# SwiGLU expansions: products of 512 columns into a pair of banks, from the fourth chunk on

## The chip, the core and the metric

The kernel runs on one core of a Trainium2 chip. The metric is the device time in microseconds. Three runs of the kernel before gave 1954.67 us as their median (1953.87 to 1956.11).

## What is computed

The reference is a stack of transformer-like blocks over 256 positions of width 1024 in fp32: two layers of a first kind (attention and gated linear attention, a recurrent mixer, convolution FFNs) and then two layers of a second kind. The change touches the second kind only, and there the two SwiGLU networks of each layer:

```python
def swiglu(h, w_gate_up, w_down):
    gu = h @ w_gate_up                      # 1024 -> 2 x 2816
    g, u = jnp.split(gu, 2, axis=-1)
    return (jax.nn.silu(g) * u) @ w_down    # 2816 -> 1024

for l in range(DEPTH):                      # DEPTH = 2
    h = swiglu(rms_norm_2(x, ffn1_pre[l]), ffn1_w_gate_up[l], ffn1_w_down[l])
    x = x + 0.5 * rms_norm_2(h, ffn1_post[l])
    h = hybrid_mixer(rms_norm_2(x, mix_pre[l]), ...)
    x = x + rms_norm_2(h, mix_post[l])
    h = swiglu(rms_norm_2(x, ffn2_pre[l]), ffn2_w_gate_up[l], ffn2_w_down[l])
    x = x + 0.5 * rms_norm_2(h, ffn2_post[l])
```

## The kernel before

Activations lie transposed: 128 channels on the partitions, 256 positions along the free side. A layer's input is 8 such tiles (`KT`), the hidden side of a SwiGLU 22 (`FF2`).

**Weights** come as one stream of chunks in the order of use. A chunk is 16 blocks of 128x128 (1 MB): in an expansion ("up") the 8 input tiles times two output tiles, one of `g` and one of `u`. SyncE moves it into one of three raw buffers (`w_raw`), as soon as VectorE has finished with the chunk three before it. ScalarE rounds it to a high part (`w_hi`, L213), VectorE takes the rest (`w_lo`, L222); both are rings of four chunks. At the end of chunk c ScalarE rounds chunk c + 4 (`refill_hi`) and VectorE makes the rest of chunk c + 3 (`refill_lo`).

**A product** is made in three parts, since fp32 values are split into a high and a low half: high weights by high input, high weights by low input, low weights by high input. The input's halves lie side by side in `x_split` (`xs`), high then low, 256 columns each; the hidden tiles in `h_split` (`hs`) likewise. `multiply` (L240 to L242) issues three matmuls of 256 columns for each block, all into the same half of a bank: both output tiles of a chunk share one PSUM bank. `multiply_wide` (L255, L258) issues one matmul of 512 columns (high weights by both halves) and one of 256 (low weights by the high half) for each block; it needs a bank for each output tile, whose left and right halves must be added afterwards. It is used in the first three of the four column groups of the contractions ("down").

**Banks.** Four PSUM banks rotate. Each use is an event; event e waits until event e - 4 has been taken by VectorE (the semaphore `pair_taken`, which starts at 4; `taken(e)` waits for the taking of e itself).

**An up stage** has 22 chunks. The layer's norm is computed while its first three chunks are multiplied: chunks 0 and 1 go together (`alternating`, L277 and L284), chunk 2 has two small matmul groups of the norm between its blocks (L316, L338), and only then is the inverse rms (`rinv`) there, by which `take_scaled` (L296) multiplies a chunk's bank while it copies it to `scratch`. From chunk 3 on TensorE goes by `whole_pe`. ScalarE works through `up_act`: for each chunk a rounding (L213), the silu of `g` (L610) and the high half of the hidden tile two chunks back (L616). VectorE works through `up_dve`: L296, the rest (L222), silu times `u` of the chunk before (L662) and the low half of the tile two back (L668).

The four stages in question are called upA and upB, in layers 0 and 1. In the profiled execution chunk 3 of them starts at 723, 1146, 1344 and 1767 us. upA and upB are each followed by a down stage of the same name.

Of the kernel before, what the change touches and what calls it, by code (L numbers as in the profile page):

```python
# [26 lines left out]
P = 128  # L27
T = 256
# [10 lines left out]
LEVELS = 8  # L39

# [4 lines left out]
LAYER = [("upA", FF2, FF2), ("downA", 12, 7), ("bg", 4, 4), ("pool_in", 4, 4), ("cv", 8, 8),  # L45
         ("gates", 8, 8), ("conv_out", 4, 4), ("pool", 1, 4), ("pool_out", 4, 4),
         ("w_o", 4, 4), ("upB", FF2, FF2), ("downB", 12, 7)]
# [96 lines left out]
class Chunk:  # L144


    def __init__(self, phase, n, layer=0):
        self.n, self.buf = n, n % 3
        self.number = C0[phase] + n + layer * LAYER_CHUNKS
        self.slot = self.number % RING  # L150
        self.event = E0[phase] + n + layer * LAYER_EVENTS
        self.bank = self.event % BANKS

# [7 lines left out]
def program(nc, x_in, stream, par1_in, par2_in, ev_const, mask_const, mats, inv_in, out):  # L161
    with ExitStack() as ctx:
# [37 lines left out]
        pair_taken = sem("psum_pair_taken")  # L200
        const_landed = sem("const_landed")
# [47 lines left out]
        def multiply_wide(pe, c, banks, src, k0, nk, first, last, ready):  # L249

            for k in range(nk):
                pe.wait_ge(*ready(k0 + k))
                for m, bank_ in enumerate(banks):
                    b = (k * 2 + m) * P
                    pe.matmul(ps[:, bank_, :], w_hi[:, c.slot, b:b + P],  # L255
                              src[:, k0 + k, :, :].rearrange("p a t -> p (a t)"),
                              start=first and k == 0, stop=False)
                    done = pe.matmul(tile(bank_, 0), w_lo[:, c.slot, b:b + P], src[:, k0 + k, 0, :],  # L258
                                     start=False, stop=last and k == nk - 1)
            done.then_inc(chunk_done, 1)  # L260
# [32 lines left out]
        def take_scaled(dve, c, dst, tiles=2):  # L293

            dve.wait_ge(chunk_done, c.number + 1)
            dve.tensor_tensor(dst, bank(c.bank, tiles), rinv[:, :].unsqueeze(1).to_broadcast([P, tiles, T]),  # L296
                              ALU.mult).then_inc(pair_taken, 1)
# [61 lines left out]
        def pre_pe(pe, phases, tr, summed, l):  # L359

            for ph, n in phases:
                done = 0
                if ph == phases[0][0]:
                    alternating(pe, Chunk(ph, 0, l), Chunk(ph, 1, l), xs, KT,
                                lambda k: tr["hi"].count(k + 1, l), lambda k: tr["lo"].count(k + 1, l))
                    c = Chunk(ph, 2, l)
                    pe.wait_ge(pair_taken, c.event + 1)
                    pe.wait_ge(lo_ready, c.number + 1)
                    multiply(pe, c, pair_tiles(c.bank), xs, 0, KT, True, True, signal=(chunk_done, 1),
                             hooks={0: lambda: mean_pe(pe, tr, summed, l), 4: lambda: rinv_pe(pe, tr, l)})  # L370
                    done = 3
                whole_pe(pe, ph, n, l, done)

        def whole_pe(pe, ph, n, l, done=0):
            for c in chunks(ph, n, l, done):
                pe.wait_ge(pair_taken, c.event + 1)
                pe.wait_ge(lo_ready, c.number + 1)
                multiply(pe, c, pair_tiles(c.bank), xs, 0, KT, True, True, signal=(chunk_done, 1))
# [224 lines left out]

        def up_act(act, phase, n, tr, func, conv, pre, l):


            def gate(c, prev):
                s = (c.slot - prev) % RING
                act.wait_ge(*(tr["gate"].count(c.n + 1 - prev, l) if conv else taken(c.event - prev)))
# [18 lines left out]
            for c in chunks(phase, n, l):  # L628
                at = c.n
                act.wait_ge(chunk_done, c.number + 1)  # L630
                if at == 0:
# [1332 lines left out]
```

## Time and profile before

| | |
|---|---|
| Median of three runs | 1954.67 us (1953.87 to 1956.11) |
| The profiled execution, time | 1953.41 us |
| The profiled execution, span of the trace | 1951.6 us |
| TensorE matmul busy | 1880.3 us, 96% |
| TensorE weight loads busy | 1821.2 us, 93% |
| VectorE busy | 1350.0 us, 69% |
| ScalarE busy | 933.8 us, 48% |
| Granted clock of TensorE, mean over the span | 0.974 |

The span is the time from the first to the last instruction in the trace. Matmuls are pipelined: a row's duration overlaps that of its neighbours, and the pace of the engine is seen from start to start.

### The profile page before, as it was taken

To read this page: it belongs to the slowest core of one execution; us is meant where nothing else is said; L and a number is where in the kernel's file an instruction comes from. 1 tells how busy PE (TensorE), PEld (TensorE's weight loads), DVE (VectorE), ACT (ScalarE), POOL (GpSimd) and SP (SyncE) were. 2 spreads that over 40 slices of the span, in tenths; PEclk is the share of its full clock that TensorE was granted. 3 is DMA by queue.
4 is the path that set the end of the run, shared out by engine and by line. 5 is a ranking of instruction groups with operands and counts; after the bars stand their busy time and mean duration, and the time that the engine had idled before them with its cause. 6 is when DMAs were issued, how large, how long until landed. Compare 5 with 4: busy or idle time off the path is not lost.

```text
span 1951.6 us, 34117 instructions
## 1 busy us (share of the span) xinstructions
PE 1880.3 (96%) x14532; PEld 1821.2 (93%) x14532; DVE 1350.0 (69%) x1676; ACT 933.8 (48%) x1101; POOL 134.0 (7%) x119
## 2 busy tenths in 40 slices
PE   7959999998999999999999999999999999999997
PEld 7938999898999899989999999999999999999997
DVE  5796899568799566656775676657665686576564
ACT  5443665457666444444354454435444445344442
POOL 0000333000233000000300000000000020000000
PEclk9968999999999999999999999999999999989999
DMA  7312555534455545553455444553555445445551
GB/s 282 145 43 76 174 193 193 185 141 164 177 200 176 192 152 178 190 215 138 166 199 190 173 151 175 205 203 133 192 187 208 145 172 196 151 152 194 186 203 66
DMA packets 46797, 334.82 MB, mean 172 GB/s; under 512 B 5184, under 2 KB 5568, under 8 KB 6464
## 3 DMA queue, kind: packets, MB, share of 16 engines
q1 hardware_dynamic: 46512, 332.20, 47.6%
q8 instruction: 115, 1.88, 0.4%
q0 software_dynamic: 144, 0.52, 0.1%
q14 instruction: 26, 0.21, 0.0%
HBM read 331.65 MB, written 1.05 MB: 170 GB/s over the span
## 4 chain that ended last, share of the span: by engine, by line
PE 88%; DVE 7%; ACT 2%; issue 1%; DMA 1%; SPq 0%; ACTq 0%; DVEq 0%
PE psum L240 19%; PE psum L241 19%; PE psum L242 19%; PE psum L255 10%; PE psum L277 7%; PE psum L258 5%; PE psum L284 3%; DVE w_lo L222 2%; PE psum L316 1%; DVE scratch L1282 1%; PE psum L483 1%; DMA w_raw<-stream_in 1%; PE psum L486 1%; PE psum L485 1%; PE psum L338 1%
## 5 line engine op out<-in xcount | busy, mean ns | idle before, releaser
L213 ACT ACTIVATE w_hi<-w_raw 128x2048 fp32r<-128x2048 f32 x313 | 598.4, 1914 | 707.5 <-PE psum L242 451.6
L240 PE MATMUL psum<-x_split,w_hi 128*128 128x256 f32 x2984 | 848.1, 284 | 11.1 <-DVE x_split L354 10.5
L241 PE MATMUL psum<-x_split,w_hi 128*128 128x256 f32 x2984 | 845.1, 283 | 0.0
L242 PE MATMUL psum<-x_split,w_lo 128*128 128x256 f32 x2984 | 845.0, 283 | 0.0
L222 DVE TENSOR_TENSOR w_lo<-w_raw,w_hi 128x2048 fp32r<-128x2048 f32 x313 | 717.4, 2296 | 55.7 <-ACT w_hi L213 55.7
L240 PEld LDWEIGHTS psum<-x_split,w_hi 128*128 128x128 f32 x2984 | 573.5, 192 | 12.3 <-issue 11.2
L241 PEld LDWEIGHTS psum<-x_split,w_hi 128*128 128x128 f32 x2984 | 573.6, 192 | 0.1
L242 PEld LDWEIGHTS psum<-x_split,w_lo 128*128 128x128 f32 x2984 | 573.4, 192 | 0.0
L296 DVE TENSOR_TENSOR scratch<-psum,inv_rms 128x512 f32<-128x512 f32 (+1 forms) x205 | 139.6, 687 | 240.7 <-PE psum L242 240.5
L255 PE MATMUL psum<-h_split,w_hi 128*128 128x512 f32 x816 | 288.6, 399 | 0.0
L258 PE MATMUL psum<-h_split,w_lo 128*128 128x256 f32 x816 | 229.2, 281 | 0.0
L255 PEld LDWEIGHTS psum<-h_split,w_hi 128*128 128x128 f32 x816 | 153.4, 188 | 38.0
L258 PEld LDWEIGHTS psum<-h_split,w_lo 128*128 128x128 f32 x816 | 154.2, 189 | 0.0
L240 PE MATMUL psum<-h_split,w_hi 128*128 128x256 f32 x448 | 126.9, 283 | 2.0 <-issue 2.0
L241 PE MATMUL psum<-h_split,w_hi 128*128 128x256 f32 x448 | 126.8, 283 | 0.0
L242 PE MATMUL psum<-h_split,w_lo 128*128 128x256 f32 x448 | 126.8, 283 | 0.0
L678 DVE SCALAR_TENSOR_TENSOR scratch<-scratch,params 128x255 f32<-128x255 f32 x192 | 120.5, 687 | 5.0 <-ACT scratch L624 4.3
L543 DVE COPY scratch<-psum 128x256 f32<-128x256 f32 (+1 forms) x42 | 18.3, 459 | 119.4 <-PE psum L258 67.4
L277 PE MATMUL psum<-x_split,w_hi 128*128 128x256 f32 x288 | 82.6, 318 | 9.5 <-ACT x_split L349 9.5
L240 PEld LDWEIGHTS psum<-h_split,w_hi 128*128 128x128 f32 x448 | 86.0, 192 | 2.5 <-issue 2.2
L242 PEld LDWEIGHTS psum<-h_split,w_lo 128*128 128x128 f32 x448 | 86.0, 192 | 0.0
L241 PEld LDWEIGHTS psum<-h_split,w_hi 128*128 128x128 f32 x448 | 86.0, 192 | 0.0
(204 smaller groups left out, 1892.7 us busy)
## 6 DMA issues: line engine op xcount, KB each, us to landing
w_raw<-stream_in SPq DMA_DIRECT2D x313, 1024.0 KB, 4.8
x_resid<-x_in SPq DMA_DIRECT2D x1, 1024.0 KB, 7.0
y_out<-x_resid SPq DMA_DIRECT2D x4, 256.0 KB, 2.5
scratch<-mask_in SPq DMA_DIRECT2D x1, 768.0 KB, 10.9
scratch<-ev_in SPq DMA_DIRECT2D x1, 512.0 KB, 9.5
scratch<-inv_in POOLq DMA_DIRECT2D x1, 512.0 KB, 3.9
params<-par_in SPq DMA_DIRECT2D x1, 247.0 KB, 7.1
matrices<-mat_in SPq DMA_DIRECT2D x1, 192.0 KB, 8.9
```

What stands on the lines that cost most here:

```text
L213: act.activation(w_hi[:, n % RING, :], raw[:, n % RAWS, :], ACT.Copy).then_inc(hi_ready, 1)
L222: dve.tensor_tensor(w_lo[:, n % RING, :], raw[:, n % RAWS, :], w_hi[:, n % RING, :].bitcast(F32), ALU.subtract).then_inc(lo_ready, 1)
L240: pe.matmul(dst, w_hi[:, c.slot, b:b + P], src[:, k0 + k, 0, :], start=opens, stop=False)
L241: pe.matmul(dst, w_hi[:, c.slot, b:b + P], src[:, k0 + k, 1, :], start=False, stop=False)
L242: done = pe.matmul(dst, w_lo[:, c.slot, b:b + P], src[:, k0 + k, 0, :], start=False, stop=last and k == nk - 1 and m == len(tiles_) - 1)
L255: pe.matmul(ps[:, bank_, :], w_hi[:, c.slot, b:b + P], src[:, k0 + k, :, :].rearrange("p a t -> p (a t)"), start=first and k == 0, stop=False)
L258: done = pe.matmul(tile(bank_, 0), w_lo[:, c.slot, b:b + P], src[:, k0 + k, 0, :], start=False, stop=last and k == nk - 1)
L277: pe.matmul(tile(c.bank, m), w[:, c.slot, b:b + P], src[:, k0 + k, 0, :], start=k == 0 and m == 0 and w is w_hi, stop=False)
L284: done = pe.matmul(tile(c.bank, m), w_hi[:, c.slot, b:b + P], src[:, k0 + k, 1, :], start=False, stop=k == nk - 1 and m == 1)
L296: dve.tensor_tensor(dst, bank(c.bank, tiles), rinv[:, :].unsqueeze(1).to_broadcast([P, tiles, T]), ALU.mult).then_inc(pair_taken, 1)
L316: ins = pe.matmul(ps[:, 7, h:h + 1], part[:, h * P:(h + 1) * P], ONES[:, 0:1], start=opens and n == 0 and h == 0, stop=closes and n == len ...
L678: dve.scalar_tensor_tensor(out=scr[:, ACC + 2 * s + t, d:T], in0=scr[:, PRE + 2 * s + t, 0:T - d], scalar=conv[0][:, bass.ds(((c.n - prev) ...
```

## The change

In the up stages of the second block (`WIDE`), chunks 3 to 21 (`NARROW = 3`) are multiplied with `multiply_wide` instead of `multiply`. Such a chunk takes two events and so two banks. When it is done, ScalarE copies the right halves of both banks into `scratch` (`ACC`, semaphore `up_right`), VectorE adds them to the left halves and releases both banks, and then multiplies the sum by `rinv` in place (semaphore `up_scaled`). The silu of a wide chunk waits for `up_scaled`. Chunks 0 to 2, the first block's expansions and all other stages are as they were.

```diff
+NARROW = 3
+WIDE = ("upA", "upB")
...
-LAYER = [("upA", FF2, FF2), ("downA", 12, 7), ...
+LAYER = [("upA", FF2, 2 * FF2 - NARROW), ("downA", 12, 7), ...
...
-        self.event = E0[phase] + n + layer * LAYER_EVENTS
+        self.wide = phase in WIDE and n >= NARROW
+        self.event = E0[phase] + n + layer * LAYER_EVENTS + (n - NARROW if self.wide else 0)
         self.bank = self.event % BANKS
+        self.last = self.event + 1 if self.wide else self.event
...
         def take_scaled(dve, c, dst, tiles=2):
 
             dve.wait_ge(chunk_done, c.number + 1)
+            if c.wide:
+                dve.wait_ge(up_right, wide_count(c))
+                dve.tensor_tensor(dst, ps[:, c.bank:c.bank + 2, 0:T], S(ACC + 2 * c.slot, 2),
+                                  ALU.add).then_inc(pair_taken, 2)
+                dve.wait_ge(*taken(c.last))
+                dve.tensor_tensor(dst, dst, rinv[:, :].unsqueeze(1).to_broadcast([P, 2, T]),
+                                  ALU.mult).then_inc(up_scaled, 1)
+                return
...
         def whole_pe(pe, ph, n, l, done=0):
             for c in chunks(ph, n, l, done):
-                pe.wait_ge(pair_taken, c.event + 1)
+                pe.wait_ge(pair_taken, c.last + 1)
                 pe.wait_ge(lo_ready, c.number + 1)
-                multiply(pe, c, pair_tiles(c.bank), xs, 0, KT, True, True, signal=(chunk_done, 1))
+                whole(pe, c)
+
+        def whole(pe, c, hooks={}):
+            if c.wide:
+                multiply_wide(pe, c, (c.bank, c.bank + 1), xs, 0, KT, True, True, hooks=hooks)
+            else:
+                multiply(pe, c, pair_tiles(c.bank), xs, 0, KT, True, True, signal=(chunk_done, 1), hooks=hooks)
...
+        def scaled(c):
+            if c.wide:
+                return up_scaled, wide_count(c)
+            return taken(c.event)
...
-                act.wait_ge(*(tr["gate"].count(c.n + 1 - prev, l) if conv else taken(c.event - prev)))
+                act.wait_ge(*(tr["gate"].count(c.n + 1 - prev, l) if conv else scaled(Chunk(phase, c.n - prev, l))))
...
             for c in chunks(phase, n, l):
                 at = c.n
                 act.wait_ge(chunk_done, c.number + 1)
+                if c.wide:
+                    act.activation(S(ACC + 2 * c.slot, 2), ps[:, c.bank:c.bank + 2, T:2 * T], ACT.Copy)\
+                       .then_inc(up_right, 1)
```

How the instructions stand now. VectorE at the start of upA in layer 0, before, from the first taking after the norm on; L296 is the multiply out of PSUM, L222 the low weights, L662 and L668 the hidden tile:

```order
L296 TENSOR_TENSOR scratch<-psum,inv_rms 128x512 [waits chunk_multiplied,normA_stat]
L296 TENSOR_TENSOR scratch<-psum,inv_rms 128x512 [waits chunk_multiplied] x2
L222 TENSOR_TENSOR w_lo<-w_raw,w_hi 128x2048 [waits chunk_hi_ready]
L662 TENSOR_TENSOR scratch<-scratch 128x256 [waits upA_act_ready] x2
L668 TENSOR_TENSOR h_split<-scratch,h_split 128x256 [waits upA_hi_ready]
L296 TENSOR_TENSOR scratch<-psum,inv_rms 128x512 [waits chunk_multiplied]
L222 TENSOR_TENSOR w_lo<-w_raw,w_hi 128x2048 [waits chunk_hi_ready]
```

And the same place now; the line numbers are those of the changed kernel, and `up_right_halves_copied` is ScalarE's copy:

```order
L313 TENSOR_TENSOR scratch<-psum,inv_rms 128x512 [waits chunk_multiplied,normA_stat]
L313 TENSOR_TENSOR scratch<-psum,inv_rms 128x512 [waits chunk_multiplied] x2
L228 TENSOR_TENSOR w_lo<-w_raw,w_hi 128x2048 [waits chunk_hi_ready]
L695 TENSOR_TENSOR scratch<-scratch 128x256 [waits upA_act_ready] x2
L701 TENSOR_TENSOR h_split<-scratch,h_split 128x256 [waits upA_hi_ready]
L307 TENSOR_TENSOR scratch<-psum,scratch 128x512 [waits up_right_halves_copied,chunk_multiplied]
L310 TENSOR_TENSOR scratch<-scratch,inv_rms 128x512 [waits psum_pair_taken]
L228 TENSOR_TENSOR w_lo<-w_raw,w_hi 128x2048 [waits chunk_hi_ready]
```

The first three chunks are taken as before; from chunk 3 on two instructions stand where one stood, ahead of the low weights.

ScalarE at the same place, chunks 2 and 3, before:

```order
L213 ACTIVATE w_hi<-w_raw 128x2048 [waits chunk_landed_1,chunk_multiplied]
L610 ACTIVATE scratch<-scratch 128x256 [waits psum_pair_taken]
L616 ACTIVATE h_split<-scratch 128x256 [waits upA_hidden_ready]
L213 ACTIVATE w_hi<-w_raw 128x2048 [waits chunk_landed_2,chunk_multiplied]
L610 ACTIVATE scratch<-scratch 128x256 [waits psum_pair_taken]
```

And now:

```order
L219 ACTIVATE w_hi<-w_raw 128x2048 [waits chunk_landed_1,chunk_multiplied]
L640 ACTIVATE scratch<-scratch 128x256 [waits psum_pair_taken]
L646 ACTIVATE h_split<-scratch 128x256 [waits upA_hidden_ready]
L662 ACTIVATE scratch<-psum 128x512 [waits chunk_multiplied]
L219 ACTIVATE w_hi<-w_raw 128x2048 [waits chunk_landed_2]
L640 ACTIVATE scratch<-scratch 128x256 [waits up_pair_scaled]
```

The copy (L662) stands ahead of the rounding, and the silu (L640) waits for VectorE's second step.

## Rows read from the trace of the kernel before

**Rows 1.** The page: busy time by engine, and the chain that ended last.

```profile
PE 1880.3 (96%) x14532; PEld 1821.2 (93%) x14532; DVE 1350.0 (69%) x1676; ACT 933.8 (48%) x1101; POOL 134.0 (7%) x119
...
PE 88%; DVE 7%; ACT 2%; issue 1%; DMA 1%; SPq 0%; ACTq 0%; DVEq 0%
```

**Rows 2.** Busy time by stretch, inside upA, layer 0; last: clock, DMA share, GB/s.

```profile
735.00:830.00 95.00, 95.00 (x794) 95.00 (x793) 59.70 (x66) 42.95 (x51) 0.00 (x0) 1.00 0.53 185
```

**Rows 3.** All waits of the same stretch: total us, times, longest.

```profile
ACT w_hi L213 <- PE psum L242: 55.0, 17, 3.2
DVE scratch L296 <- PE psum L242: 37.4, 17, 2.2
```

**Rows 4.** Timeline, TensorE (start us, us): chunk 3 and the down stage's first matmul.

```profile
723.39 0.28 PE L240 MATMUL psum<-x_split,w_hi 128*128 128x256 f32 x1
...
832.83 0.40 PE L255 MATMUL psum<-h_split,w_hi 128*128 128x512 f32 x1
...
1145.64 0.28 PE L240 MATMUL psum<-x_split,w_hi 128*128 128x256 f32 x1
...
1255.08 0.40 PE L255 MATMUL psum<-h_split,w_hi 128*128 128x512 f32 x1
...
1767.03 0.28 PE L240 MATMUL psum<-x_split,w_hi 128*128 128x256 f32 x1
...
1876.47 0.40 PE L255 MATMUL psum<-h_split,w_hi 128*128 128x512 f32 x1
```

**Rows 5.** Timeline, TensorE, down stage of layer 0 and the end of its third group.

```profile
847.32 0.40 PE L255 MATMUL psum<-h_split,w_hi 128*128 128x512 f32 x1
847.56 0.28 PE L258 MATMUL psum<-h_split,w_lo 128*128 128x256 f32 x1
847.67 0.40 PE L255 MATMUL psum<-h_split,w_hi 128*128 128x512 f32 x1
...
879.47 0.28 PE L240 MATMUL psum<-h_split,w_hi 128*128 128x256 f32 x1
879.59 0.28 PE L241 MATMUL psum<-h_split,w_hi 128*128 128x256 f32 x1
```

**Rows 6.** Groups of instructions (busy us, mean ns, idle before), shapes near the new ones.

```profile
L401 ACT ACTIVATE scratch<-x_resid 128x512 f32<-128x512 f32 x24 | 13.1, 616 | 0.0
L1020 ACT ACTIVATE scratch<-psum,params 128x256 f32<-128x256 f32 x16 | 6.2, 516 | 0.0
L1571 DVE TENSOR_TENSOR scratch<-scratch 128x512 f32<-128x512 f32 x8 | 5.5, 692 | 0.3
L1543 DVE TENSOR_TENSOR scratch<-psum,scratch 128x512 f32<-128x512 f32 x8 | 5.5, 690 | 23.1 <-PE psum L284 16.8 <-PE psum L242 6.4
```

**Rows 7.** Timeline, ScalarE, one chunk of upA, layer 0.

```profile
821.51 1.92 ACT L213 ACTIVATE w_hi<-w_raw 128x2048 fp32r<-128x2048 f32 x1 [3.23 <-PE psum L242]
823.33 0.40 ACT L610 ACTIVATE scratch<-scratch 128x256 f32<-128x256 f32 x1
```

**Rows 8.** Timeline, VectorE: an add and the one that waits for it.

```profile
708.08 0.68 DVE L429 TENSOR_TENSOR square_sum<-scratch 128x512 f32<-128x512 f32 x1
708.87 1.49 DVE L429 TENSOR_TENSOR square_sum<-square_sum,scratch 128x512 f32<-128x512 f32 x2
```

**Rows 9.** Timeline, VectorE, one chunk of upA, layer 0, and the last hidden tile.

```profile
821.51 0.69 DVE L296 TENSOR_TENSOR scratch<-psum,inv_rms 128x512 f32<-128x512 f32 x1 [2.20 <-PE psum L242]
822.12 2.28 DVE L222 TENSOR_TENSOR w_lo<-w_raw,w_hi 128x2048 fp32r<-128x2048 f32 x1
...
836.85 0.99 DVE L668 TENSOR_TENSOR h_split<-scratch,h_split 128x256 fp32r<-128x256 f32 x2
```

**Rows 10.** Transfers of the stretch 735 to 830: KB each, median us to landing.

```profile
w_raw<-stream_in SPq DMA_DIRECT2D x16, 1024.0 KB, 4.8
```

**Rows 11.** Timeline, VectorE: chunks 0 to 2 of upA, layer 0, taken.

```profile
722.38 1.90 DVE L296 TENSOR_TENSOR scratch<-psum,inv_rms 128x512 f32<-128x512 f32 x3
```

More of the change, by code:

```diff
@@ L44 @@
          ("up1", FF1, FF1), ("down1", 12, 7)]
-LAYER = [("upA", FF2, FF2), ("downA", 12, 7), ("bg", 4, 4), ("pool_in", 4, 4), ("cv", 8, 8),
+LAYER = [("upA", FF2, 2 * FF2 - NARROW), ("downA", 12, 7), ("bg", 4, 4), ("pool_in", 4, 4), ("cv", 8, 8),
          ("gates", 8, 8), ("conv_out", 4, 4), ("pool", 1, 4), ("pool_out", 4, 4),
-         ("w_o", 4, 4), ("upB", FF2, FF2), ("downB", 12, 7)]
+         ("w_o", 4, 4), ("upB", FF2, 2 * FF2 - NARROW), ("downB", 12, 7)]
 C0, E0 = {}, {}
@@ L147, in __init__ @@
     def __init__(self, phase, n, layer=0):
-        self.n, self.buf = n, n % 3
+        self.n, self.buf, self.phase, self.layer = n, n % 3, phase, layer
         self.number = C0[phase] + n + layer * LAYER_CHUNKS
         self.slot = self.number % RING
-        self.event = E0[phase] + n + layer * LAYER_EVENTS
+        self.wide = phase in WIDE and n >= NARROW
+        self.event = E0[phase] + n + layer * LAYER_EVENTS + (n - NARROW if self.wide else 0)
         self.bank = self.event % BANKS
+        self.last = self.event + 1 if self.wide else self.event
 def chunks(phase, count, layer=0, done=0):
@@ L200, in program @@
         pair_taken = sem("psum_pair_taken")
+        up_scaled = sem("up_pair_scaled")
+        up_right = sem("up_right_halves_copied")
         const_landed = sem("const_landed")
@@ L247, in multiply, with multiply_wide @@
                 done.then_inc(*signal)
-        def multiply_wide(pe, c, banks, src, k0, nk, first, last, ready):
+        def multiply_wide(pe, c, banks, src, k0, nk, first, last, ready=None, hooks={}):
             for k in range(nk):
-                pe.wait_ge(*ready(k0 + k))
+                if ready is not None:
+                    pe.wait_ge(*ready(k0 + k))
                 for m, bank_ in enumerate(banks):
@@ L259, in multiply_wide @@
                                      start=False, stop=last and k == nk - 1)
+                if k in hooks:
+                    hooks[k]()
             done.then_inc(chunk_done, 1)
@@ L366, in pre_pe @@
                     c = Chunk(ph, 2, l)
-                    pe.wait_ge(pair_taken, c.event + 1)
+                    pe.wait_ge(pair_taken, c.last + 1)
                     pe.wait_ge(lo_ready, c.number + 1)
-                    multiply(pe, c, pair_tiles(c.bank), xs, 0, KT, True, True, signal=(chunk_done, 1),
-                             hooks={0: lambda: mean_pe(pe, tr, summed, l), 4: lambda: rinv_pe(pe, tr, l)})
+                    whole(pe, c, hooks={0: lambda: mean_pe(pe, tr, summed, l), 4: lambda: rinv_pe(pe, tr, l)})
                     done = 3
@@ L375, in whole_pe @@
             for c in chunks(ph, n, l, done):
-                pe.wait_ge(pair_taken, c.event + 1)
+                pe.wait_ge(pair_taken, c.last + 1)
                 pe.wait_ge(lo_ready, c.number + 1)
-                multiply(pe, c, pair_tiles(c.bank), xs, 0, KT, True, True, signal=(chunk_done, 1))
+                whole(pe, c)
[4 more added lines that the diff above has]
+                multiply(pe, c, pair_tiles(c.bank), xs, 0, KT, True, True, signal=(chunk_done, 1), hooks=hooks)
         def post_tracks(name, layered=True):
@@ L602, in up_tracks, with wide_count @@
             return {k: Signal(sem(f"{name}_{k}_ready"), 2 * m if k == "taps" else m) for k in names}
+        def wide_count(c):
+            return (WIDE.index(c.phase) + 2 * c.layer) * (FF2 - NARROW) + c.n - NARROW + 1
+        def scaled(c):
+            if c.wide:
+                return up_scaled, wide_count(c)
+            return taken(c.event)
         def up_act(act, phase, n, tr, func, conv, pre, l):
```

## The prediction, made before the changed kernel was run

> **What bounds the kernel now.** I read the page first: TensorE is busy for 1880.3 of 1951.6 us, VectorE for 1350.0, ScalarE for 933.8, and 88% of the chain that ended last is TensorE [rows 1]. A busy share does not say which wait ends last in the part that is changed, so the second view is the stretch table inside the first changed stage, upA of layer 0. There TensorE is busy without a break, 95.00 of 95.00 us, at a granted clock of 1.00, while VectorE has 59.70 and ScalarE 42.95 us of work [rows 2]. The third view is the list of waits of the same stretch: only two kinds of waits stand there, and in both another engine waits for TensorE [rows 3]. So in this stage the time is the number of TensorE instructions times their spacing, and nothing else, as long as the others stay in time.
>
> **What a product costs, from start to start.** A matmul's own 0.28 us in the rows overlaps its neighbours, so I take starts. Chunk 3 of the stage (the first that is changed) begins at 723.39 and the down stage's first matmul at 832.83 [rows 4]. Between them lie 19 chunks of 16 blocks (8 input tiles by 2 output tiles), each block three products of 256 columns: 109.44 / 19 = 5.760 us a chunk, / 16 = 0.3600 us a block, 0.120 us a product. The other three stages read the same: 1145.64 to 1255.08 for the second and 1767.03 to 1876.47 for the fourth, 109.44 us each [rows 4], and the third likewise. So there is no stall in any of the four that the change could take away; it can gain only by a cheaper block.
>
> The down stage right behind is already written in the new form, one product of 512 columns and one of 256 for a block. Its first three groups run from 832.83 to 879.47 [rows 4, 5]: 46.64 us for 3 groups x 22 tiles x 2 = 132 blocks, 0.3533 us a block. One period can be read singly: 847.32, 847.56, 847.67, that is 0.24 and 0.11 to 0.12 us [rows 5]. The number of streamed columns is 768 in both forms; what goes is one instruction and one weight load a block.
>
> **The change part by part.**
>
> TensorE, the gain. 4 stages x 19 chunks x 16 blocks = 1216 blocks; the order listing has 1216 products of 512 columns on x_split where before had 2 x 1216 of 256. Each saves 0.3600 - 0.3533 = 0.0067 us: 0.107 us a chunk (5.760 to 5.653), 2.03 us a stage, **8.1 us in all**. Both figures are from blocks that read the same kind of ring slots and the same layout of high and low halves; only the moving buffer differs (x_split for h_split). The bounds of this term: nothing saved, 0.3600; and on the other side the 768 columns alone at the granted full clock, 2.4 GHz, 0.320 us, which would save 48.6 us. The down stage's row is the same code (multiply_wide) with the same shapes, so I take 0.3533.
>
> What the skill would make of it: the Trainium skill, page "TensorE: Matmul & The Clock Gate", section "Back-to-back issue gap", gives a warm matmul N / 2.4 + 2.5 ns. By that a dropped instruction returns only its fixed 2.5 ns, 1216 x 2.5 ns = 3.0 us in all, an estimate from that page. The trace disagrees with the page: 256 columns take 120 ns here and not 109, and the pair returns 6.7 ns.
>
> ScalarE, one more instruction a chunk: the copy of the right halves, 128x512 out of PSUM. No such row is there; the nearest are a 128x512 activation out of SBUF, 616 ns, and a 128x256 one out of PSUM, 516 ns [rows 6]. I take 0.61, bounds 0.52 and 1.0 (twice the smaller). In the steady stage ScalarE is idle for 3.23 us of each 5.76 [rows 7], so this is hidden; the copy stands ahead of the rounding of the next weights (w_hi, L213) and delays it by about 0.5 us. Behind that stands the silu (L610), which now waits for VectorE's second step; it comes up 0.61 + 1.82 = 2.4 us after the old start of the rounding [rows 7], and VectorE's result is there by 2.3 (below).
>
> VectorE: L296 (one multiply by the inverse rms out of PSUM) becomes an add of PSUM and scratch and a multiply in scratch, both 128x512: 690 and 692 ns [rows 6]. The multiply waits for the add itself. Such a dependent step costs 0.79 us from start to start (708.08 to 708.87) [rows 8], where L222 follows L296 after 0.61 [rows 9]. Of that 0.11 lies between the end of the one and the start of the other, and I take it for the copy's signal too. So, counted from where L296 started before: the copy 0.61 and its signal 0.11, then the add (ends at 1.41), the multiply 0.79 after its start (ends at 2.20), w_lo 0.61 behind that, 0.72 + 0.79 + 0.61 = 2.12 us where it was 0.61. VectorE is later by 1.51 us a chunk. It was idle for 2.20 us a chunk [rows 9], and the chunk is 0.11 shorter: 0.58 us of idle is left. So it keeps up, without a backlog that grows. What is queued behind the new wait: w_lo of the chunk three further on, the product of silu and up (L662), and the low half of the hidden tile (L668).
>
> Who waits for that. (1) The banks: a wide chunk takes two of the four, so chunk n needs the add of chunk n-2, which ends 1.41 us after that chunk's end and is wanted 5.65 after it. (2) w_lo: made at a chunk's end for the chunk that starts two chunks later, 11.3 us; it is ready after 4.4. (3) The raw weights: their buffer is freed 1.51 us later. Before, w_lo ended at 824.40 [rows 9], a transfer lands 4.8 us on [rows 10], 829.2, and the rounding that wants it is two chunks after 821.51 [rows 7], 833.03: 3.8 us to spare, and then 3.8 - 1.51 - 0.21 + 0.61 = 2.7. (4) The down stage: it wants the last hidden tile (k = 21) at its 43rd block, 847.67 [rows 5]; VectorE made it by 836.85 + 0.99 = 837.84 [rows 9], now about 1.5 later, 8 us ahead. All four are hidden; cost 0.
>
> The start of the stage. Chunk 3 used to wait for a bank of the stage before; now it needs two banks and so the taking of chunk 0. VectorE does that first of three, from 722.38 [rows 11], so until about 723.07, and chunk 3 starts at 723.39 [rows 4], its first weights 0.12 earlier: 0.2 us to spare. That is the thinnest place. Cost 0 as read; at the other bound TensorE runs dry for 0.3 us and picks up again, in four stages 1.2 us. Chunk 4 needs chunk 2, taken by 722.38 + 1.90 = 724.28 [rows 11], 5 us ahead.
>
> Fewer instructions and another parity of the banks in later stages: the banks only rotate, and nobody waits for them there beyond the same chain; 0.
>
> **Sum.** The profiled execution: 1953.41 us around a span of 1951.6. Less 8.1: 1945.3 and 1943.5. The median of the runs, 1954.67, lies 1.26 above the profiled one; less 8.1 it is **1946.6**.
>
> **The rivals.**
>
> A. A block with x_split as the moving operand costs more than 0.3568 us, so that less than 3.9 us is left. For it: no row shows 512 columns of x_split, and the up stage has more reads of PSUM by the other engines. Against it: in products of 256 columns x_split and h_split cost the same, 0.120 us (879.47 to 879.59 [rows 5] beside the 0.120 of the up stage), with and without a wait for each tile. The mechanism would be that the dropped instruction returns only part of the 13 ns by which 120 exceeds 256 columns at full clock. Between 1950.8 and 1954.7; if it returned only a fifth, 1216 x 0.0026 = 3.2, 1951.5. By the page's rule above the time would be 1951.6. Chance 6%, since 132 blocks beside it show the whole 6.7.
>
> B. Slower: VectorE becomes the bound of the wide chunks. It decides where its chain for a chunk is over 5.65 us; my sum is 5.07 (5.76 - 2.20 + 1.51). A lateness L per chunk adds up over 19 chunks; the first 4.2 us of it (5.65 - 1.41) are taken up before chunk n waits for the add of n-2. To turn the gain of 8.1 into a loss of 3.9, 3.0 us a stage must be lost: 19 L = 7.2, L = 0.38, a chain of 6.0 us, 1.0 more than the rows give: a copy that takes 1.6 us, or a multiply with a broadcast operand in place at over twice its 0.69. The time would be 1958.6 or more. Against it: all of these operations have rows of nearly the same shape. 3%.
>
> C. TensorE stalls at chunk 3 because the taking of chunk 0 is 0.2 us too close: 0.3 to 0.6 us in each of four stages, 1947.8 to 1949.0. Inside the forecast's range, still faster. 12% of the 90% below.
>
> D. Much faster, towards 0.320 us a block: 1% or less, since the down rows are the same code. That the change does not do what it says is excluded by the listing.
>
> **How the numbers follow.** Forecast 1946.6 with its variants 90%, A 6%, B 3%, D 1%. The forecast's own width: the runs before spread over 2.2 us (1953.87 to 1956.11), so 1.1 to each side for the median and as much for the 8.1, and C on the upper side: 1944.3 to 1950.0. That holds about 88%, and I leave A and B out. A measurement of this kernel can tell about 0.2%, 3.9 us, from no change: faster by more than that is under 1950.8, so 91%; within it 6%; slower 3%.
>
> **What would show it.** Right: in the four up stages from chunk 3 on, 0.353 us a block and 5.65 us a chunk, 107.4 us from chunk 3 to the down stage; TensorE busy throughout; new rows of about 0.61 us on ScalarE and 0.69 twice on VectorE; VectorE idle ahead of the add for 0.6 us a chunk by its own queue plus the wait for the copy; every later stage of unchanged length and only shifted by 2, 4, 6 and 8 us. Wrong: a block of 0.357 or more (A); rows in which TensorE waits for the add of VectorE in the middle of a stage (B) or once at chunk 3 (C); a ScalarE wait for a transfer in the up stages, which has none now.

## The result and the profile after

The changed kernel takes **1940.91 us** (three runs, 1940.50 to 1941.37) where the kernel before took 1954.67: ratio 0.9933, 95% interval 0.9913 to 0.9952. The forecast was 1946.6 with a range of 1944.3 to 1950.0. It is faster, as forecast, but by 13.8 us in place of 8.1, and below the range. The profiled execution took 1940.91 us around a span of 1939.1, 12.5 us less than that of before (1953.41, 1951.6). Among all later runs, two executions were slower by far more than any other (one of `before_late4`, 2273.85 us, and one of the kernel before beside it, 3634.54), and they are left out of every median here.

The page of the changed kernel, busy time by engine (beside [rows 1]), then the stretch table inside upA of layer 0, beside [rows 2], and all waits from 726 to 830 us, beside [rows 3]:

```profile
PE 1868.7 (96%) x13316; PEld 1751.0 (90%) x13316; DVE 1403.1 (72%) x1752; ACT 971.5 (50%) x1177; POOL 133.7 (7%) x119
```

```profile
735.00:830.00 95.00, 95.00 (x540) 82.42 (x540) 71.27 (x84) 51.20 (x68) 0.00 (x0) 1.00 0.53 188
```

```profile
ACT scratch L662 <- PE psum L265: 46.1, 18, 2.7
DVE scratch L307 <- ACT scratch L662: 24.6, 18, 1.4
DVE h_split L701 <- ACT h_split L646: 1.0, 1, 1.0
```

TensorE is still busy for 95.00 of 95.00 us, VectorE now for 71.27 and ScalarE for 51.20, and apart from TensorE only ScalarE is waited for, by VectorE: in each chunk for the copy, 1.37 us (24.6 / 18), and once for a hidden tile. The timeline of TensorE at chunk 3 of that stage, at the end of the stage, and where the third group of the down stage ends, beside [rows 4, 5] (start us, duration us):

```profile
724.22 0.28 PE L248 MATMUL psum<-x_split,w_lo 128*128 128x256 f32 x1
724.34 0.40 PE L262 MATMUL psum<-x_split,w_hi 128*128 128x512 f32 x1
...
831.64 0.28 PE L265 MATMUL psum<-x_split,w_lo 128*128 128x256 f32 x1
831.75 0.40 PE L262 MATMUL psum<-h_split,w_hi 128*128 128x512 f32 x1
...
878.39 0.28 PE L246 MATMUL psum<-h_split,w_hi 128*128 128x256 f32 x1
```

From chunk 3 to the down stage it is 831.75 - 724.34 = 107.41 us, 0.3533 us a block; the forecast said 107.4 and 0.353. The other three stages read 107.41, 107.42 and 107.41. Chunk 3 starts 0.12 us behind the last product of chunk 2 in all four, so there is no stall. VectorE and ScalarE in one chunk of the same stage, beside [rows 9] and [rows 7]:

```profile
815.72 0.69 DVE L307 TENSOR_TENSOR scratch<-psum,scratch 128x512 f32<-128x512 f32 x1 [1.36 <-ACT scratch L662]
816.45 0.69 DVE L310 TENSOR_TENSOR scratch<-scratch,inv_rms 128x512 f32<-128x512 f32 x1
817.06 2.28 DVE L228 TENSOR_TENSOR w_lo<-w_raw,w_hi 128x2048 fp32r<-128x2048 f32 x1
```

```profile
814.99 0.60 ACT L662 ACTIVATE scratch<-psum 128x512 f32<-128x512 f32 x1 [2.64 <-PE psum L265]
815.49 1.91 ACT L219 ACTIVATE w_hi<-w_raw 128x2048 fp32r<-128x2048 f32 x1
817.30 0.40 ACT L640 ACTIVATE scratch<-scratch 128x256 f32<-128x256 f32 x1
```

The copy takes 0.60 us (forecast 0.61). The add starts 0.73 behind its start (0.72), the multiply 0.73 behind that (0.79), and w_lo 2.07 us after the copy's start (2.12). All of it is hidden.

**Where the other 4.4 us of the profile are.** Between two stages lies a *norm passage*: behind the last product of the contraction come the norm's own small matmuls and the first two chunks of the next stage, which TensorE takes as their inputs arrive. I count it from the start of TensorE's last product of the contraction to the start of its first product of chunk 2. There are six of them behind each other from 698 us on, before and after built alike. This is the stretch table of the six of before; the numbers behind the colon are the length, and the third from the end is the mean granted clock:

```profile
698.11:716.31 18.20, 15.82 (x111) 15.38 (x110) 13.37 (x23) 7.87 (x15) 0.00 (x0) 0.81 0.15 46
896.08:914.21 18.13, 15.78 (x112) 15.34 (x111) 15.27 (x28) 8.28 (x15) 0.00 (x0) 0.81 0.02 3
1120.12:1138.56 18.44, 16.09 (x112) 15.76 (x110) 15.98 (x28) 8.28 (x15) 0.00 (x0) 0.81 0.06 13
1318.33:1336.65 18.32, 15.97 (x111) 15.64 (x110) 15.87 (x28) 8.27 (x15) 0.00 (x0) 0.81 0.05 8
1516.42:1534.69 18.27, 15.92 (x111) 15.59 (x110) 15.82 (x28) 8.27 (x15) 0.00 (x0) 0.81 0.03 4
1740.72:1759.95 19.23, 16.88 (x111) 16.45 (x110) 15.85 (x28) 8.27 (x15) 0.00 (x0) 0.73 0.05 9
```

And the same six of the changed kernel:

```profile
699.14:717.26 18.12, 15.74 (x111) 15.30 (x110) 13.37 (x23) 7.87 (x15) 0.00 (x0) 0.81 0.13 45
895.00:912.26 17.26, 14.91 (x112) 14.58 (x111) 14.80 (x28) 8.28 (x15) 0.00 (x0) 0.90 0.00 1
1118.10:1136.31 18.21, 15.86 (x112) 15.53 (x111) 15.75 (x28) 8.29 (x15) 0.00 (x0) 0.81 0.06 15
1314.05:1331.91 17.86, 15.52 (x111) 15.08 (x110) 14.89 (x28) 8.28 (x15) 0.00 (x0) 0.81 0.01 1
1509.65:1526.78 17.13, 14.78 (x111) 14.45 (x110) 14.67 (x28) 8.27 (x15) 0.00 (x0) 0.90 0.00 1
1732.73:1749.43 16.70, 13.95 (x112) 13.24 (x110) 14.24 (x28) 8.29 (x15) 0.00 (x0) 1.00 0.02 8
```

The work is the same before and after: 110 to 112 matmuls, ScalarE's 7.87 to 8.29 us. Only the first passage differs from the other five, in both kernels: VectorE has 23 instructions in it and not 28. The length follows the clock: 19.2 us at 0.73, 17.9 to 18.4 at 0.81, 17.1 to 17.3 at 0.90, 16.7 where the clock stays at its full level of 2.4 GHz. Before, the six take 110.59 us in sum and after 105.28: 5.3 us less. The balance of the profiles: up stages -8.1, passages -5.3, what lies ahead of the first passage +1.0 (699.14 for 698.11), together -12.4 of the 12.5.

Each such table is of one execution, and the medians are over several. So the question for the runs was why the passages are shorter. Theory 1: what part of a passage runs at the low clock (1.2 GHz) depends on when it comes, and the change only moved the passages. Theory 2: the wide form itself shortens them.

### The profile page after: what moved, and what is told of

Same layout as the page of the kernel before. It is cut to its first block, busy times and chain, and to the rows that moved or that the text cites. A ratio compares the mean times of both kernels' runs of the same rounds, so it can differ in the third digit from the quotient of the medians.

```text
span 1939.1 us, 31837 instructions
## 1 busy us (share of the span) xinstructions
PE 1868.7 (96%) x13316; PEld 1751.0 (90%) x13316; DVE 1403.1 (72%) x1752; ACT 971.5 (50%) x1177; POOL 133.7 (7%) x119
## 4 chain that ended last, share of the span: by engine, by line
PE 88%; DVE 7%; ACT 2%; issue 1%; DMA 1%; SPq 0%; DVEq 0%; ACTq 0%
PE psum L262 25%; PE psum L265 12%; PE psum L246 12%; PE psum L247 12%; PE psum L248 12%; PE psum L286 7%; PE psum L293 3%; DVE w_lo L228 2%; PE psum L333 1%; PE psum L505 1%; DVE scratch L1315 1%; PE psum L508 1%; PE psum L507 1%; DMA w_raw<-stream_in 1%; PE psum L355 1%
## 5 line engine op out<-in xcount | busy, mean ns | idle before, releaser
L246 PE MATMUL psum<-x_split,w_hi 128*128 128x256 f32 x1768 | 504.2, 285 | 11.2 <-DVE x_split L371 10.7
L247 PE MATMUL psum<-x_split,w_hi 128*128 128x256 f32 x1768 | 501.1, 283 | 0.0
L262 PE MATMUL psum<-x_split,w_hi 128*128 128x512 f32 x1216 | 429.8, 399 | 0.0
L246 PEld LDWEIGHTS psum<-x_split,w_hi 128*128 128x128 f32 x1768 | 340.1, 192 | 12.6 <-issue 11.5
L247 PEld LDWEIGHTS psum<-x_split,w_hi 128*128 128x128 f32 x1768 | 340.3, 192 | 0.1
L262 PEld LDWEIGHTS psum<-x_split,w_hi 128*128 128x128 f32 x1216 | 228.5, 188 | 56.9
L262 PEld LDWEIGHTS psum<-h_split,w_hi 128*128 128x128 f32 x816 | 153.3, 188 | 38.2
L265 PEld LDWEIGHTS psum<-h_split,w_lo 128*128 128x128 f32 x816 | 154.2, 189 | 0.0
L313 DVE TENSOR_TENSOR scratch<-psum,inv_rms 128x512 f32<-128x512 f32 (+1 forms) x129 | 87.0, 684 | 79.4 <-PE psum L248 79.2
L662 ACT ACTIVATE scratch<-psum 128x512 f32<-128x512 f32 x76 | 45.5, 598 | 193.8 <-PE psum L265 193.8
L307 DVE TENSOR_TENSOR scratch<-psum,scratch 128x512 f32<-128x512 f32 x76 | 52.6, 692 | 103.2 <-ACT scratch L662 103.2
```

The source lines that it names most:

```text
L246: pe.matmul(dst, w_hi[:, c.slot, b:b + P], src[:, k0 + k, 0, :], start=opens, stop=False)
L247: pe.matmul(dst, w_hi[:, c.slot, b:b + P], src[:, k0 + k, 1, :], start=False, stop=False)
L262: pe.matmul(ps[:, bank_, :], w_hi[:, c.slot, b:b + P], src[:, k0 + k, :, :].rearrange("p a t -> p (a t)"), start=first and k == 0, stop=False)
L307: dve.tensor_tensor(dst, ps[:, c.bank:c.bank + 2, 0:T], S(ACC + 2 * c.slot, 2), ALU.add).then_inc(pair_taken, 2)
L662: act.activation(S(ACC + 2 * c.slot, 2), ps[:, c.bank:c.bank + 2, T:2 * T], ACT.Copy)\
```

## The experiments

Each group of runs has the kernel before beside it, on the same chip, and every ratio is taken to that. Its medians on the five chips: 1953.90 (again, wide_padded, before_late8 and 16), 1953.10 (hold and only), 1953.85 (light, narrow13, wide_late16), 1953.42 (before_late4, 12 and 20, wide_late8) and 1954.81 (before_late24, wide_late24). "Six passages" is always the sum of the table above, from that kernel's own profile.

**The changed kernel again.**

> The changed kernel as it is, run again. The up stages gave 8.1 us in its first profile, the five passages between stages in which a norm is computed 5.2 us more (the granted clock was higher in them). Theory 1 (the clock): the passages take 16.7 to 19.2 us each by how much of each runs at the low clock, and that may come out otherwise from run to run: up stages again 107.4 us from chunk 3 to the down stage, the whole 1938 to 1950. Theory 2 (the wide form itself shortens the passages): the five passages again at their 87.2 us in sum, the whole within 1 us of 1940.9.

1941.99 us (1940.47 to 1942.61, five runs), ratio 0.9942 (0.9928 to 0.9955): 11.9 us under the kernel beside it. Up stages as before to 0.07 us. Six passages 104.72 us, but not the same ones: the third took 16.70 in place of 18.21 and the fourth 18.16 in place of 17.86. So one and the same kernel meets other clocks from run to run. The profiled execution was the fastest of the five (1940.47).

**A shift ahead of the passages.** Idle products of 256 columns into a bank that nobody uses, before chunk 3 of upA in layer 0; everything later comes later. N is 4, 8, 12, 16, 20 or 24 in the kernel before and 8, 16 or 24 in the changed one (`filler` is the loop over the idle products):

```diff
+PAD = {('upA', 0): N}
...
+        def filler(pe, count, number, src):
+            for _ in range(count):
+                pe.matmul(tile(4, 0), w_hi[:, number % RING, 0:P], src[:, 0, 0, :], start=True, stop=True)
...
                 pe.wait_ge(lo_ready, c.number + 1)
+                if c.n == 3:
+                    filler(pe, PAD.get((ph, l), 0), c.number, xs)
```

> The kernel before with 4 idle products (0.48 us) ahead of chunk 3 of upA in layer 0. Open is whether the wide form gains in the passages by more than the chance of when they come. Theory 1 (chance alone): over the shifts of 0, 0.48, 0.96, 1.44, 1.92, 2.40 and 2.88 us the kernel before, less its shift, spreads around 1951 to 1952, 8 us over the changed kernel's mean over its own shifts; so some of the new shifts are at 1950 or below. This one 1950 to 1955. Theory 2 (the wide form helps in the passages too): the mean of before stays at 1953.5, over 10 us above.

> The kernel before with 8 idle products (0.96 us) ahead of chunk 3 of upA in layer 0 alone, everything later shifted by that. Theory 1: the passages after it change by some tenths up to 2.5 us each, in either direction, and the whole is 1948 to 1958, not 0.96 over before. Theory 2 (only the form of the up chunks matters): 1954.67 + 0.96 = 1955.6, passages as before within 0.1 us.

> 12 idle products (1.44 us). 8 gave 1952.2 and 16 gave 1957.3. Theory 1: between, 1952 to 1958; the mean over the shifts decides. Theory 2 the same for this one alone.

> As the one with 8, with 16 idle products (1.92 us). Theory 1: again other lengths of the passages, other than with 8; the whole 1948 to 1958. Theory 2: 1954.67 + 1.92 = 1956.6, passages as before.

> 20 idle products (2.40 us). Theory 1: 1953 to 1959, less its shift 1951 to 1957. The mean over the shifts decides between the theories.

> 24 idle products (2.88 us) in the kernel before. Theory 1 (chance of when the passages come): 1952 to 1958. The mean over the shifts, less the shift, decides: 8 us over the changed kernel's mean by theory 1, 10 or more by theory 2 (the wide form makes low stretches rarer).

| kernel | shift us | median us | less the shift | beside the unshifted one | six passages us |
|---|---|---|---|---|---|
| before | 0 | 1953.90 | 1953.90 | 0 | 110.59 |
| before_late4 | 0.48 | 1952.23 | 1951.75 | -1.7 | 109.75 |
| before_late8 | 0.96 | 1952.22 | 1951.26 | -2.6 | 109.04 |
| before_late12 | 1.44 | 1952.97 | 1951.53 | -1.9 | 109.12 |
| before_late16 | 1.92 | 1957.33 | 1955.41 | +1.5 | 111.86 |
| before_late20 | 2.40 | 1956.17 | 1953.77 | +0.4 | 110.49 |
| before_late24 | 2.88 | 1955.14 | 1952.26 | -2.5 | 110.77 |

With 0.96 us of added work the kernel before is not slower (ratio 0.9992, 0.9983 to 1.0001), with 1.92 it is 3.4 us slower (1.0019, 1.0010 to 1.0028). These two ran on one chip, ten times each, and don't overlap: 1950.35 to 1954.07 and 1956.03 to 1959.97, 5.1 us between the medians for 0.96 us of work. Less the shift the medians spread over 4.1 us, though nothing was changed but when the later work comes. Two passages of the kernel with 8 and one of that with 16, as the table above has them:

```profile
895.87:913.11 17.24, 14.89 (x111) 14.56 (x110) 14.78 (x28) 8.28 (x15) 0.00 (x0) 0.90 0.00 1
1739.16:1758.33 19.17, 16.93 (x111) 16.50 (x110) 15.80 (x28) 8.28 (x15) 0.00 (x0) 0.73 0.06 12
```

```profile
1123.56:1142.88 19.32, 16.97 (x112) 16.53 (x111) 15.96 (x28) 8.28 (x15) 0.00 (x0) 0.73 0.05 9
```

In these executions the second passage took 17.24 us for the 18.13 of before, at a clock of 0.90, and the third 19.32 for 18.44, at 0.73. Both belong to kernels without a wide up chunk: theory 2 is not needed for a passage of 17.2 us.

> The changed kernel with 8 idle products (0.96 us). Unshifted it is 1942.0, with 1.92 us 1944.2. Theory 1: 1942 to 1947, and the mean of the changed kernel over its shifts comes to 8 us under the mean of before. Theory 2: 1942.9.

> The changed kernel with 16 idle products (1.92 us) ahead of chunk 3 of upA in layer 0 alone. Theory 1 (the changed kernel's passages come at times at which little of them runs at the low clock, and a shift spoils that): more than 1942.0 + 1.9 = 1943.9, up to 1948, with longer passages. Theory 2 (the wide form shortens the passages itself): 1943.9, passages as in the changed kernel.

> 24 idle products (2.88 us) in the changed kernel. Theory 1: 1943 to 1949, with passages of other lengths than unshifted. Theory 2: 1942.0 + 2.9 = 1944.9.

| kernel | shift us | median us | less the shift | beside the kernel before | six passages us |
|---|---|---|---|---|---|
| changed (again) | 0 | 1941.99 | 1941.99 | -11.9 | 104.72 |
| wide_late8 | 0.96 | 1943.93 | 1942.97 | -10.4 | 107.60 |
| wide_late16 | 1.92 | 1944.18 | 1942.26 | -11.6 | 106.73 |
| wide_late24 | 2.88 | 1944.99 | 1942.11 | -12.7 | 106.94 |

The passages are longer in all three profiles with a shift, by 2.0 to 2.9 us beside `again` and by 1.5 to 2.3 beside the first profile of the changed kernel; theory 2 had them unchanged. One of them, the third of `wide_late8`, is a wide kernel's passage at the clock of 0.73:

```profile
1120.17:1139.46 19.29, 16.94 (x111) 16.50 (x110) 15.92 (x28) 8.28 (x15) 0.00 (x0) 0.73 0.07 14
```

It takes 19.29 us where the narrow kernel above took 19.32 in the same place: at an equal clock the wide form shortens nothing there. But the medians moved by little more than the shift, which is what theory 2 said, though with four runs each their ratios are known to 3 or 4 us to each side only. And the means over all shifts lie 1952.8 - 1942.3 = 10.5 us apart, not 8: here theory 1 in its plain form missed. What the tables show of it: the last of the six passages took 19.10 to 19.25 us in all seven kernels of the first table, and 16.69 or 16.70 in three of the four of the second (18.12 with 24). So the shifts did not average over all clocks there, and between the last passages alone 2.4 to 2.6 us are left in most pairs. A reason may be that each passage before it is itself stretched or not; no run shows it.

**All runs at an equal clock.** Each run has its mean granted clock beside its time. These are the means of all runs of the kernel before (shifted or not, less the shift) and of the changed one, by that clock:

| mean clock | before: runs, mean us | changed: runs, mean us | apart |
|---|---|---|---|
| 0.973 | 40, 1954.95 | none | |
| 0.974 | 23, 1953.46 | none | |
| 0.975 | 20, 1952.54 | 1, 1943.25 | 9.3 |
| 0.976 | 26, 1951.82 | 5, 1942.57 | 9.3 |
| 0.977 | 14, 1951.20 | 6, 1942.49 | 8.7 |
| 0.978 | 8, 1949.46 | 3, 1941.58 | 7.9 |
| 0.980 | 1, 1947.69 | 1, 1939.77 | 7.9 |

The 23 runs of before at 0.970 to 0.972 and the 4 of the changed kernel at 0.979 have nothing beside them. One straight line for each kernel, with a common slope, through all 175 runs gives 1.0 us for 0.001 of mean clock, and 8.5 us between the kernels at an equal clock (8.0 to 8.9; an estimate from these runs): the 8.1 of the up stages. So what the changed kernel gains beyond them goes with a higher clock, on average 0.977 for 0.974. Why it meets the low clock less often this does not say.

**The wide form with the distances of the kernel before.** The changed kernel, with 17 idle products ahead of chunk 3 in each of the four up stages (17 x 0.12 = 2.04 us, what the stage saves):

```diff
+PAD = {('upA', 0): 17, ('upA', 1): 17, ('upB', 0): 17, ('upB', 1): 17}
```

> The changed kernel with 17 idle products of 256 columns into an unused bank ahead of chunk 3 in each of the four up stages: 17 x 0.120 = 2.04 us each, 8.16 in all, so that every later stage comes at the distances of the kernel before. Theory 1 (the clock depends on when a passage comes): the passages come out much as before, 18.1 to 19.2 us, and the time is 1952 to 1955. Theory 2 (the wide form itself shortens the passages): they stay at 16.7 to 18.2 us and the time is 1940.9 + 8.2 = 1949.1.

1951.90 us (1949.99 to 1955.77, ten runs), ratio 0.9996 (0.9987 to 1.0005): the whole gain is gone within the noise, the 8.16 us of the stages and all or most of what lay beside them. By the medians 2.0 us are left; that is 0.1 below what theory 1 said, while the 1949.1 of theory 2 lies outside the interval. Six passages 107.36 us in its profile, which was the fastest of the ten. Where before had 0.73 and 19.23 us for the last, it has:

```profile
1738.75:1756.01 17.26, 14.91 (x112) 14.58 (x110) 14.81 (x28) 8.28 (x15) 0.00 (x0) 0.90 0.03 11
```

Less its 8.16 us it would be 1943.7, 1.4 above the mean of the changed kernel over its shifts; and it is 0.9 under the mean of the kernel before over its own.

**A part of the change alone.** Wide chunks in upA only, in upB only (`WIDE` cut to one name, and that stage's events alone doubled; where a pair would begin in bank 3 it reaches into bank 4, unused there), and from chunk 13 on in both (`NARROW = 13`).

> The wide form in upA of both layers alone, upB as before (where a pair would begin in bank 3 it reaches into bank 4, which is unused there). In the stages themselves 2 x 2.03 = 4.05 us less. Theory 1: the whole is 1953.9 - 4.05 = 1949.8 plus or minus up to 4 us from the passages. Theory 2: half of the 5.2 us comes with it, 1947.2.

> The wide form in upB of both layers alone. In the stages 4.05 us less. Theory 1: 1949.8 plus or minus up to 4 us, and not the same as with upA alone, since other passages are shifted. Theory 2: 1947.2, the same as upA alone.

> The wide form from chunk 13 on in place of chunk 3: 9 wide chunks in each of four stages, 4 x 9 x 16 x 0.0067 = 3.8 us less in the stages themselves (113.3 - 3.84 / 4, that is 108.5 us from chunk 3 to the down stage). Theory 1: the whole 1953.5 - 3.8 = 1949.7, plus or minus up to 4 us from the passages. Theory 2 (a gain in the passages that comes with the wide form): half of 5.2 us more, 1947.

From chunk 2's start to the down stage an up stage takes 116.52 us in the kernel before and 114.49 to 114.56 in the changed one. With upA alone the four read 114.49, 116.52, 114.49, 116.52; with upB alone 116.52, 114.49, 116.52, 114.49; from chunk 13 on 115.56 each, 0.96 less (9 x 0.107). So the saving in a stage is exactly additive: 0.107 us a wide chunk. The medians: 1947.41 (ratio 0.9964, 0.9950 to 0.9978), 1947.65 (0.9968, 0.9956 to 0.9980) and 1948.83 (0.9976, 0.9966 to 0.9985), that is 5.7, 5.5 and 5.0 us, where the stages give 4.05, 4.05 and 3.84. The rest, 1.2 to 1.6 us, is less than the intervals of these ratios (1.9 to 2.7 us to each side); the passages of the three profiles are shorter too (107.93, 108.91 and 109.63 us). Theory 2 said 1947.2, 1947.2 and 1947, near the first two; theory 1 had them inside its width. These three don't tell the theories apart.

**The clock held up.** The same filler where TensorE waits in each passage, ahead of the wait for the inverse rms and behind it, in the kernel before and in the changed one. First 12 and 16 products, then 6 and 10:

```diff
+                more = c.number + 1 < CHUNKS
+                if more:
+                    pe.wait_ge(lo_ready, c.number + 2)
+                    filler(pe, 12, c.number + 1, hs)
                 rinv_pe(pe, post, l)
+                if more:
+                    filler(pe, 16, c.number + 1, hs)
```

> The kernel before with idle products of 256 columns into an unused bank while TensorE waits in each of the six norm passages: 12 ahead of the wait for the inverse rms (1.44 of 1.79 us) and 16 behind it (1.92 of 2.37 us). Theory 1 (the granted clock in these passages is what made the 5.2 us): the low stretches go, each passage takes about 16.7 us, which is what the one passage without a low stretch took, 100 us for six in place of 110.6, and the time falls by about 10 to 1943 to 1945. If the filler only delays the norm's own products, the time rises instead. Theory 2 (the wide form itself shortens the passages): passages stay at 18.1 us and more, 1953 to 1955.

> The same filler in the changed kernel. Theory 1: with the clock held in both, only the cheaper blocks are left between them: 8.1 us below the kernel before with the filler, about 1935.5. Theory 2: the gap between the two stays at 11 to 13 us, since the wide form shortens the passages whatever the clock.

1952.65 us (ratio 0.9993, 0.9983 to 1.0002) and 1943.65 (0.9947, 0.9930 to 0.9964). The gain of 10 us that was expected did not come: low stretches were rarer, but the filler itself held the passages up. Two of the kernel before with it:

```profile
1122.03:1140.80 18.77, 18.37 (x139) 17.96 (x138) 14.24 (x28) 8.29 (x15) 0.00 (x0) 0.91 0.01 3
1320.63:1338.03 17.40, 16.88 (x139) 16.41 (x138) 14.23 (x28) 8.29 (x15) 0.00 (x0) 1.00 0.00 0
```

At the full clock 17.40 in place of 16.70 us, and 18.77 where part of it was low. So fewer idle products:

> The kernel before with a lighter filler, 6 idle products ahead of the wait for the inverse rms and 10 behind it, so that they fit into the waits (1.79 and 2.37 us) at the low clock too (0.213 us each there: 1.28 and 2.13). In the heavier form the filler itself held the passage up by 0.7 us with the clock high (17.41 in place of 16.70) and by more with it low. Theory 1: passages of 16.7 us where the clock stays up, 17.2 with a short low stretch; the whole 1943 to 1950. If the lighter filler no longer keeps the clock up, the passages read as without it, 1951 to 1956.

> The lighter filler in the changed kernel. Theory 1: 8.1 us below the kernel before with the same filler, plus or minus what the passages of the two differ by in their low stretches (each to be read from its profile): 1935 to 1941.

The kernel before with the lighter filler: **1945.57 us** (ratio 0.9961, 0.9947 to 0.9975), 8.3 us less without any change in its stages. Its second to sixth passage:

```profile
894.09:910.78 16.69, 15.68 (x127) 15.04 (x126) 14.24 (x28) 8.28 (x15) 0.00 (x0) 1.00 0.01 1
1116.87:1134.36 17.49, 17.00 (x128) 16.54 (x126) 14.24 (x28) 8.29 (x15) 0.00 (x0) 0.90 0.02 6
1314.18:1330.88 16.70, 15.68 (x127) 15.04 (x126) 14.24 (x28) 8.28 (x15) 0.00 (x0) 1.00 0.00 1
1510.72:1527.42 16.70, 15.69 (x128) 15.05 (x126) 14.24 (x28) 8.28 (x15) 0.00 (x0) 1.00 0.00 1
1733.47:1750.17 16.70, 15.69 (x128) 15.05 (x126) 14.25 (x28) 8.27 (x15) 0.00 (x0) 1.00 0.02 6
```

The changed kernel with it: **1937.94 us** (1936.87 to 1941.15, ratio 0.9920, 0.9903 to 0.9937), the fastest of all, 15.9 us under the kernel before. Its last two passages:

```profile
1508.01:1524.70 16.69, 15.69 (x127) 15.05 (x126) 14.24 (x28) 8.28 (x15) 0.00 (x0) 1.00 0.01 2
1730.64:1747.33 16.69, 15.70 (x127) 15.05 (x126) 14.23 (x28) 8.29 (x15) 0.00 (x0) 1.00 0.02 8
```

At the full clock each of the second to sixth passages takes 16.69 to 16.70 us in both kernels, and the changed one takes the same without a filler (its last passage above), so the wide form shortens no passage by itself. Six passages 101.51 and 100.11 us. The first passage is a shorter one, as this execution of the changed kernel shows, the only one with the full clock there:

```profile
701.70:717.61 15.91, 15.27 (x127) 15.01 (x126) 13.14 (x23) 7.88 (x15) 0.00 (x0) 1.00 0.06 10
```

It begins at 701.70, where the other 19 profiles have 697.1 to 699.1: executions differ ahead of the passages too, where both kernels are alike.

With the clock mostly held in both, the medians are 1945.57 - 1937.94 = 7.6 us apart, near the 8.1 of the up stages, and with the heavier filler 9.0. With four to ten runs each this is loose: by the intervals of the ratios it may be 4 to 12 us and 5 to 13. It agrees with the 8.5 at an equal clock; alone it would not exclude the 12 us of the kernels as they are.

## Why the prediction missed

**Right.** The block: 0.3533 us as read from the down stage, 107.41 us a stage for the forecast 107.4, in all four; rival A (a dearer block with x_split) is out. The dropped instruction returned 6.7 ns in these stages, and not the 2.5 of the rule that the prediction set beside its sum. The Trainium skill, page "TensorE: Matmul & The Clock Gate", section "Back-to-back issue gap", gives that rule for a single product by itself, and says that in a stream of weight loads and products both set the spacing; these stages are such a stream, so they contradict the prediction's use of the rule and not the page. The work of ScalarE and VectorE: 0.60 for 0.61, and w_lo 2.07 us behind the copy's start for 2.12; rival B (VectorE as the bound) is out with VectorE 75% busy in the stage (71.27 of 95). Rival C, the thin place at chunk 3: no stall in any stage. The additivity, by the three partial kernels. So the mechanism that was forecast is the one that the stages show; it is the rest of the kernel that was taken to stand still.

**Wrong.** The step that failed is the last one, "every later stage of unchanged length and only shifted by 2, 4, 6 and 8 us". In the sum it was a term that stood at 0: what the shift does to the passages. It measured -5.3 us in the profiles. The width failed for the same reason: I took 1.1 us from the spread of three runs of one kernel, where a shift alone moves the kernel before from -2.6 to +1.5 us. It could have been read: the table of times had the mean clock at 0.974, below 1.00, and the stretch table over the six passages, which I did not ask for, shows six almost equal pieces of work that take 18.13 to 19.23 us at clocks of 0.81 and 0.73. What they take at the full clock only the later runs showed, 15.91 for the first and 16.70 for each of the others, 99.4 in all; so 11.2 us of the kernel before hung on the clock. That is the bound that the range lacked below: 1946.6 - 11.2 = 1935.4, an estimate.

**What is shown and what stays open.** Shown: the length of a passage goes with its granted clock, alike in both kernels (16.7 us at the full clock, 19.3 at 0.73); a shift without any wide chunk changes the kernel by other than its own length, either way; and at an equal mean clock the two kernels are 8.5 us apart, which is what the stages give. Not settled: why the changed kernel meets the low clock less often, so that over the shifts it is 10.5 us faster and not 8. With the distances of before it is as slow as before within the noise (0.9987 to 1.0005), so the distances between the passages explain most of it. But the last passage never got better than 19.10 us in the seven kernels without wide chunks that are shifted by the first stage alone, and took 17.26 in the padded one, in one profiled execution each. That the measured 13.8 us fell outside the range is thus in part luck: the forecast left out a term whose sign the rows before did not show, and it fell on the fast side.

## What to carry to other kernels

Where a stage is bound by TensorE without a gap, as these were, the saving of a cheaper block could be read off a neighbouring stage to a tenth of a microsecond, and it was additive. But before a change of a few microseconds is believed, or missed, look at the granted clock in each place where TensorE pauses: such places give and take microseconds when they are merely moved, so price them at both clocks and widen the range by them. To compare two versions, set runs of an equal mean clock side by side, or hold the clock in both with idle products that fit into the waits even at the low clock; in this kernel that was also worth about 4 us on top of the change (1941.99 to 1937.94, on two chips).

## What the runs showed of the hardware

- In a passage TensorE stands still twice, in the fourth one of the kernel before for 0.55 and 1.66 us. Around these waits the granted clock fell to the lower of its levels, 1.2 GHz, and stayed there into the products behind them; not each time: without a filler four to all six of the passages had such a stretch, with the lighter filler two and one. The cost in the second to sixth passage was 0.4 to 0.7 us at a mean clock of 0.90, 1.1 to 1.9 at 0.81 and 2.4 to 2.6 at 0.73. Which wait brings the clock down the traces don't show. In the last passage of before it fell at 1741.2, ahead of both waits:

```profile
1741.20:1751.40 10.20, 7.85 (x35) 7.42 (x35) 7.51 (x18) 4.06 (x10) 0.00 (x0) 0.50 0.00 0
```

- The Trainium skill, page "TensorE: Matmul & The Clock Gate", section "What's actually happening", says that the watching of activity runs freely and isn't reset by a kernel's start. The runs agree in that the same kernel met other clocks in its third and fourth passage when it was run again.
- 16 idle products of 256 columns in a passage (6 and 10) cost nothing at the full clock (16.70 us with and without), 28 cost 0.7 us.
- A product of 512 columns and one of 256, each with its weight load, took 0.3533 us from start to start with x_split and with h_split alike, with a wait for each tile or without: 0.0067 us less than three of 256 (0.3600).
- A VectorE operation of 128x512 that waits for the one before it started 0.73 us behind it in the chunk shown (815.72 to 816.45), and 0.79 in [rows 8]; one that does not, 0.61 (816.45 to 817.06).
